# Two-layer decoder trunk: the seven products of a gate step paired by gate and up, their sums chained in place, down in two groups, and the parts of x in two rounds

## The reference, cut to what matters

```python
def swiglu(h, w_gate, w_up, w_down):
    return (jax.nn.silu(h @ w_gate) * (h @ w_up)) @ w_down

for l in range(DEPTH):
    x = x + 0.5 * swiglu(rms_norm(x, g_ffn1[l]), w_ffn1_gate[l], w_ffn1_up[l], w_ffn1_down[l])
    h = rms_norm(x, g_mix[l])
    # l == 0: x = x + conv_gating_mixer(h, ...)    l == 1: x = x + stick_breaking_mixer(h, ...)
    x = x + 0.5 * swiglu(rms_norm(x, g_ffn2[l]), w_ffn2_gate[l], w_ffn2_up[l], w_ffn2_down[l])
return rms_norm(x, g_final)
```

## Time and profile before

| | |
|---|---|
| median of 3 runs | 2059.07 us (2058.8 to 2063.93) |
| profiled execution, its own time | 2057.78 us |
| its span | 2056.1 us |
| PE busy, share of the span | 92% |
| DVE, ACT, POOL busy | 70%, 42%, 36% |
| mean granted PE clock | 0.956 of full |

### The profile page before, as it was taken

The page is one execution under the profiler, slowest core; times in us unless marked ns, Lnnn a source line. Parts: engine busy times, 40 slices in busy tenths (PEclk is TensorE's granted clock), DMA queues, the critical chain, the costliest instruction groups (busy, mean ns, idle before and its releaser), DMA issues.

```text
span 2056.1 us, 30552 instructions
## 1 busy us (share of the span) xinstructions
PE 1893.6 (92%) x11779; PEld 1696.5 (83%) x11779; DVE 1441.8 (70%) x1410; ACT 854.0 (42%) x1028; POOL 744.2 (36%) x551
## 2 busy tenths in 40 slices
PE   2999999989877999999599999989999969999998
PEld 2999988767657999988599998867888859999886
DVE  7778774579878778844977785453666697878642
ACT  3445442313235545522444543223555445544422
POOL 6454510331454555201645430040333274555003
PEclk6999999999988999999899999989999979999998
DMA  5788932222135888523479863223111147798321
GB/s 135 163 174 173 187 122 92 72 82 82 42 82 124 175 181 176 153 92 95 100 170 178 186 141 122 70 65 102 42 41 42 42 102 163 163 189 181 113 82 41
DMA packets 390330, 243.35 MB, mean 118 GB/s; under 512 B 13980, under 2 KB 358624, under 8 KB 390256
## 3 DMA queue, kind: packets, MB, share of 16 engines
q1 hardware_dynamic: 297088, 196.13, 32.1%
q0 software_dynamic: 93056, 46.22, 18.1%
q10 hardware_dynamic: 112, 0.03, 0.0%
HBM read 240.22 MB, written 2.10 MB: 118 GB/s over the span
## 4 chain that ended last, share of the span: by engine, by line
PE 69%; DVE 18%; issue 6%; POOL 4%; ACT 3%; DMA 0%; DVEq 0%; POOLq 0%; ACTq 0%
PE ps L360 23%; PE ps L362 22%; PE ps L361 22%; DVE w_lo L1361 5%; DVE y L1598 2%; ACT w_hi L978 2%; POOL ssq L1872 2%; POOL sq L1870 1%; PE ps L827 1%; PE ps L821 1%; DVE act_in L1397 1%; DVE xs_lo L1518 1%; DVE act_in L1402 1%; DVE x_sums L1501 1%; DVE w_lo L1332 1%
## 5 line engine op out<-in xcount | busy, mean ns | idle before, releaser
L360 PE MATMUL ps<-xs_hi,w_hi 128*128 128x256 f32 x2464 | 708.1, 287 | 110.6 <-DVE w_lo L1361 67.6
L361 PE MATMUL ps<-xs_lo,w_hi 128*128 128x256 f32 x2464 | 700.7, 284 | 0.0
L362 PE MATMUL ps<-xs_hi,w_lo 128*128 128x256 f32 x2464 | 700.4, 284 | 0.0
L1361 DVE TENSOR_TENSOR w_lo<-stage,w_hi 128x1024 fp32r<-128x1024 f32 x264 | 397.9, 1521 | 361.7 <-ACT w_hi L1051 200.8
L360 PEld LDWEIGHTS ps<-xs_hi,w_hi 128*128 128x128 f32 x2464 | 471.1, 191 | 122.3 <-DVE w_lo L1361 51.8
L361 PEld LDWEIGHTS ps<-xs_lo,w_hi 128*128 128x128 f32 x2464 | 471.4, 191 | 1.0 <-issue 1.0
L362 PEld LDWEIGHTS ps<-xs_hi,w_lo 128*128 128x128 f32 x2464 | 471.4, 191 | 0.0
L978 ACT ACTIVATE w_hi<-stage 128x1024 fp32r<-128x1024 f32 x176 | 182.7, 1057 | 306.0 <-PE ps L362 289.0
L1870 POOL TENSOR_TENSOR sq<-x_res 128x512 f32<-128x512 f32 x55 | 79.7, 1450 | 573.9 <-DVE x_res L1347 565.8
L360 PE MATMUL ps<-h_split,w_hi 128*128 128x512 f32 x704 | 278.8, 396 | 0.0
L361 PE MATMUL ps<-h_split,w_hi 128*128 128x512 f32 x704 | 278.7, 396 | 0.0
(11 more groups left out here) (229 smaller groups left out, 3024.2 us busy)
## 6 DMA issues: line engine op xcount, KB each, us to landing
stage<-in_w_ffn_gate_dram SPq DMA_DIRECT2D x176, 256.0 KB, 3.3
stage<-in_w_ffn_up_dram SPq DMA_DIRECT2D x176, 256.0 KB, 3.8
stage<-in_w_ffn_down_dram SPq DMA_DIRECT2D x176, 256.0 KB, 2.9
stage<-in_w_ffn_gate_dram POOLq DMA_DIRECT2D x88, 256.0 KB, 6.1
stage<-in_w_ffn_up_dram POOLq DMA_DIRECT2D x88, 256.0 KB, 6.8
stage<-in_w_qkv_dram SPq DMA_DIRECT2D x24, 512.0 KB, 4.9
sums<-in_w_ffn_gate_dram SPq DMA_DIRECT2D x44, 256.0 KB, 3.2
sums<-in_w_ffn_up_dram SPq DMA_DIRECT2D x44, 256.0 KB, 5.1
```

Source lines behind the costliest of these rows:

```text
L360: pe.matmul(to, a_hi, b_hi, start=start, stop=False, skip_group_check=True)
L361: pe.matmul(to, a_hi, b_lo, start=False, stop=False, skip_group_check=True)
L362: return pe.matmul(to, a_lo, b_hi, start=False, stop=stop, skip_group_check=True)
L1361: dve.tensor_tensor(w_lo[:, slot, :], src, w_hi[:, slot, :].bitcast(F32), ALU.subtract).then_inc(item_lo_made, 1)
```

## The change

It does the following things, together:

- **Output halves.** The second halving of a step is now gate against up, no longer first against last hidden channels; a step makes hidden tiles 2f and 2f+1. Each weight block is one DMA of 512 KB with rows of 1 KB, where there were two of 256 KB with rows of 512 B. The contraction is halved into even and odd tiles, so pairs of x are tiles 2k and 2k+1.
- **Order of the items:** T1, W11, T3, W21, T2, W22, T4. The gate half is complete after W22, so scale_gate and the silu come before T4 is done in all but the first step.
- **Sums.** T1 lies in one of two buffers (chain): SP loads W11's block there, POOL's DMA adds W12. T2 and T4 are made by POOL in the same buffer, in place, so each waits until the item before it in the chain has been split (item_lo_made). T3 is W12 plus W22 by an accumulating DMA.
- **Down in two groups of four output tiles.** An entry is two rows by four tiles (24 matmuls again). Entries 0 to 10 finish tiles 0 to 3, entries 11 to 21 tiles 4 to 7, and the residuals of the first group are added at entry 13. The high and low parts of hid are made anew in the second group, in two buffers that are parts S2 and S4 of x. PE's down loop is written out. The squares (POOL) or parts of x (ACT, DVE) for tiles 0 to 3 are made at entries 14 and 15.
- **Parts of x in two rounds.** x_pair makes five of seven parts; x_rest makes S2 and S4 for all four pairs afterwards.
- **Squares before an FFN** are taken by ACT (x_square, 128x512) and only added by POOL. Before the mixers and the final norm POOL still does both.

The diff, cut to its core:

```diff
-W11, W21, T1, T3, T2, W22, T4 = range(ITEMS)
+T1, W11, T3, W21, T2, W22, T4 = range(ITEMS)
-TAIL = [2, 3, 2, 2]
+GROUP = 4
+TAIL = 2
...
+        def gate_block(n, item, step):
+            w = ffn_weights[n][0 if item in (T3, W22) else 1]
+            odd = int(item in (W21, W22))
+            return w.rearrange("(k two p) f -> p two k f", two=2, p=P)[:, odd, :, bass.ds(step.count(2 * P, 0), 2 * P)]
...
 (load_ffn, SP)
+                for f in range(1, HF):
+                    if f > 1:
+                        sp.wait_ge(item_lo_made, lo0 + ITEMS * (f - 2) + T4 + 1)
+                        load_chain(n, Step(f))
+                    for item in (W11, T3, W21, W22):
+                        sp.wait_ge(item_lo_made, lo0 + ITEMS * (f - 1) + item + 1)
+                        if item == W21:
+                            sp.wait_ge(t4_made, n * HF + f)
+                        elif item == W22:
+                            sp.wait_ge(t2_made, n * HF + f)
+                        load_block(n, item, Step(f))
...
 (gate_first, PE)
+                pe.wait_ge(xs_lo_made, 10 * n + 2 * KH + 1)
+                gate_item(n, step, T2)
+                pe.wait_ge(xs_lo_made, 10 * n + 2 * KH + 2)
+                gate_item(n, step, W22)
                 pe.wait_ge(ssq_added, (norm + 1) * DT)
+                sum_squares(stats_bank(n)).then_inc(ssq_summed, 1)
+                gate_item(n, step, T4)
...
 (gate_mid and gate_step, ACT)
+                copy_r0(n, step)
+                hi(n, step, T2)
+                copy_v0(n, step)
+                hi(n, step, W22)
+                hi(n, step, T4)
...
+                if not step.first():
+                    hi(n, step, T3)
+                    hi(n, step, W21)
+                gate_mid(n, step)
+                copy_v(n, step)
+                hi(n, step.next(), T1)
+                if step.first():
+                    token_rms(NORM_FFN[n], stats_bank(n))
+                hi(n, step.next(), W11)
+                silu(n, step)
...
 (ffn(1) after down, ACT)
+                    first_hi(2, T1)
+                    first_hi(2, W11)
+                    x_pair(2, 2)
+                    first_hi(2, T3)
+                    first_hi(2, W21)
+                    x_pair(2, 3)
+                    x_rest(2)
+                    for j in range(GROUP, DT):
+                        x_square(2, j)
...
 (gate_step, DVE)
+                if not step.first():
+                    lo(n, step, T3)
+                    make_hid(n, Step(step.f - 1, step.i))
+                    lo(n, step, W21)
+                lo(n, step, T2)
+                lo(n, step, W22)
+                s57(n, step)
+                lo(n, step, T4)
+                c11(n, step)
+                c22(n, step)
+                lo(n, step.next(), T1)
+                c12(n, step)
+                if step.first():
+                    lo(n, step.next(), W11)
+                    c21(n, step)
+                    invert_rms(NORM_FFN[n])
+                    scale_gate(n, step)
+                else:
+                    scale_gate(n, step)
+                    lo(n, step.next(), W11)
+                    c21(n, step)
...
 (down, DVE)
+                for e in range(2, FT):
+                    if e + 1 < HF:
+                        scale_hid(n, e + 1)
+                    hid_lo(n, e)
+                    if e + 2 < FT:
+                        row_lo(n, e + 2)
+                    if e == 13:
+                        for at in range(GROUP):
+                            residual(n, at)
...
 (POOL)
+            def add_t4(n, step):
+                pool.wait_ge(item_lo_made, step.count(ITEMS, n * FFN_ITEMS + T2 + 1))
+                pool.wait_ge(raw_loaded[RAW_OF[W21]], step.count(16, raw_count(n, RAW_OF[W21]) + 16))
+                pool.tensor_tensor(step.chain(), step.chain(), raw(step, W21), ALU.add).then_inc(t4_made, 1)
+            def add_first(n):
+                add_t1(n, Step(0))
+                add_t3(n, Step(0))
+                if n:
+                    for j in range(GROUP):
+                        add_square(n, j)
+                add_t2(n, Step(0))
+                add_t1(n, Step(1))
+                for j in range(GROUP if n else 0, DT):
+                    add_square(n, j)
+                add_t4(n, Step(0))
+                add_t3(n, Step(1))
+            def gate_step(n, step):
+                add_t2(n, step)
+                if step.f < HF - 1:
+                    add_t1(n, step.next())
+                add_t4(n, step)
+                if step.f < HF - 1:
+                    add_t3(n, step.next())
```

More of the change, by code:

```diff
@@ L1416, in gate_step @@
             def gate_step(n, step):
+                if not step.first():
+                    lo(n, step, T3)
[5 more added lines that the diff above has]
+                lo(n, step, T4)
                 c11(n, step)
-                lo(n, step, W22)
-                lo(n, step, T4)
-                s57(n, step)
-                lo(n, step.next(), W11)
@@ L1926, in ffn @@
[L1926 to L1927 removed]
+                for f in range(1, HF):
+                    gate_step(n, Step(f))
+                clear_ssq(norm + 1)
+                if n == 1:
+                    add_first(2)
+                else:
+                    for j in range(DT if n < 3 else DT - 1):
+                        square_tile(norm + 1, j)
             def mask_diagonals(of, compare, count_sem):
@@ L1947, in _ @@
             clear_ssq(0)
-            squares(0, PAIRED, 0)
+            add_first(0)
             ffn(0)
@@ L1993, in _ @@
             clear_ssq(2)
-            squares(2, IN_ORDER, 1)
+            add_first(1)
             ffn(1)
@@ L2006, in _ @@
             clear_ssq(5)
-            squares(5, IN_ORDER, 3)
+            add_first(3)
             ffn(3)
```

843 lines of the change are left out of this document (413 added, 430 removed).

## The result

The changed kernel takes 1986.6 us (median of four runs, 1986.2 to 1989.7) against 2061.5 (2058.8 to 2065.4) on the same chip: ratio 0.9638, 95% interval 0.9617 to 0.966, 75 us less. The forecast was 1992, range 1966 to 2026. A later set on another chip (run e_again) gave 1986.8 for the same kernel (five runs, 1982.7 to 1987.9), but 2051.5 for the kernel before (nine runs, 2048.6 to 2057.6): ratio 0.9675, 95% interval 0.9657 to 0.9692, 65 us less. So the change is worth 65 to 75 us, and the kernel before varies more from set to set than the changed one does. The profiled execution spans 1984.7 us where that of before spans 2056.1, so there are 71.4 us to account for.

A forecast was written before the change was run, and what follows sets the result against it. PE was busy 1893.6 of 2056.1 us, so only idle time or slow clock, mostly in passages between stages, could be won. Terms summed to -67 from the profiled 2057.78, 1991, with the median 1.3 above: 1992, range 1966 to 2026.

The forecast's parts named there:

- The first case: Whole kernel: the gains and losses come as summed, 1970 to 2015 us; chance 0.72.
- Mixers' heads: FFN 0 to conv, FFN 2 to attention: early squares end PE's 9.1 us waits for ssq; 12 and 13 us won.
- FFN 1 to FFN 2: Passage with two x pairs made before down ends; stalls at T2 (5.7 us) and T4 remain; 14 us won, bounds 8 and 18.
- Mixer to FFN 3: Passage into FFN 3: pairs 0 and 1 made under the last output tiles, x_pair 3.4 us; 9 us won, bounds 3 and 15.
- Start: FFN 0's first step: first weights no longer wait behind POOL's squares; ends about 62 instead of 68.7; 7 us won.
- Gate steps: Later FFN steps: POOL's sums stand apart where DVE has slack, so later stalls go; 12 us won, bounds 3 and 14.
- first steps: After step 0: silu(0) ahead of T3's high part makes PE's stall about 4.1 against 2.6; four times, 6 us lost.
- Down: Doubled hid work is covered except in entries 14 and 15, mainly FFN 1's; 7 us lost, bounds 0 and 12.
- DMA: SP and POOL queues: fewer, larger DMAs for the same bytes; DMA does not get worse, no term in the sum.
- the second: POOL's sums hold DVE in the steps: no gain there and 0.5 us more in each of 40, 2024; chance 0.12.
- The third: FFNs' first steps win nothing because T2 and T4 wait behind squares on ACT and POOL, 2029; chance 0.07.
- The fourth: T3's accumulating DMA lands later than its 14 us in the steps, each us then costing 40: slower; chance 0.04.

The follow-up runs named there:

- e_again: The changed kernel run once more, unaltered, beside the combined kernel on another chip: 1986.8 us (1982.7 to 1987.9).
- e_late: The changed kernel with tiles 0 to 3's residuals and all that followed at entries 13 to 15 moved behind the last down matmul: 2021.8 us.
- e_pool_sq: The changed kernel with the squares in front of the FFNs made on POOL again instead of by ACT: 2008.1 us.
- e_start: The changed kernel with pair 1 of x made ahead of T1's high part at the start, on ACT and DVE: 1981.6 us.
- e_squares: The changed kernel with ACT's squares in front of the FFNs moved into ACT's idle gaps, and POOL's adds with them: 1984.0 us.
- e_tail: The changed kernel with tiles 4 and 5 of down's row 20 taken before tile 4 of row 21: 1982.8 us.
- e_rows: The changed kernel with each SP block load as two DMAs of 256 KB with packets of 512 bytes: 2014.9 us.
- e_rows_order: The e_rows kernel, with SP loading W22 ahead of W21: 1996.9 us.
- e_pool_more: The changed kernel with two further unused sums of 512 columns on POOL behind T2's sum in each of steps 1 to 10: 2009.6 us.
- e_first: The changed kernel with step 1's T3 and W21 high parts ahead of silu(0) on ACT, T3's low part ahead of DVE's reciprocal: 1982.9 us.
- e_best1: The changed kernel with e_first, e_start and e_tail joined, squares and T2's sum placed, and step 1's T3 DMA issued earlier: 1952.5 us.

## Why the prediction was right

The first case came: 1986.6 for 1992, and the sum of -67 stands at -71 in the spans. The mechanisms came too, place by place. That the sum is so near is partly luck: the gate steps gave 10 us more than forecast and down 2.5 us less loss, FFN 1 and FFN 2 near 3 us more, and the start, the end and the way to FFN 3 some 11 us less. By its terms:

- **Mixers' heads**, -12 and -13: -11.0 and -13.2. PE's wait for ssq is gone and the clock stays at 1.00, as it said. e_late shows the cause: with the tiles late they lose 8.6 and 10.5 us again.
- **FFN 1 to FFN 2**, -14: -15.1. The stall at T2 is 4.0 us for 5.7. The second, at T4, did not appear: T2 and W22 run partly at half clock behind the first stall and give T4 its time. e_late gives 9.6 of it to the early pairs.
- **Mixer to FFN 1**, -7: -8.6. **Mixer to FFN 3**, -9: -4.6, within its bounds of 3 and 15. The step that was off is the pair at 3.4 us: pairs 0 and 1 take 2.5 us each, but pair 2 of FFN 3 takes 7.7 us (1608.29 to 1616.04), four of its six instructions at 1.54, 1.48, 1.48 and 2.83 us beside POOL's adds of squares and T2's sum. PE waits 7.5 us. Pair 2 of FFN 1 is held as long (584.45 to 592.27), but PE waits only 2.2 us for it. This was the lower bound's own condition, and e_pool_sq shows the kind of loss. One part of pair 2 on DVE, and what POOL does meanwhile:

```profile
1612.56 2.83 DVE L1575 SCALAR_TENSOR_TENSOR xs_lo<-x_res,params,xs_hi 128x512 fp32r<-128x512 f32 x1
```

```profile
1606.71 5.64 POOL L1990 TENSOR_TENSOR ssq<-ssq,copies 128x512 f32<-128x512 f32 x4 [6.28 <-ACT copies L1201]
1612.43 2.41 POOL L1978 TENSOR_TENSOR chain<-chain,stage 128x1024 f32<-128x1024 f32 x1
```

- **Start**, -7: -2.5. The count took T1's DMA as one wait of ACT, but all of pair 1 stood behind it (6.4 us; e_start wins 4.5 to 5.3 back), and ACT's eight squares and POOL's eight adds stood in front of T2 and T4 (e_squares: 4.4).
- **End**, -6: -4.2 for down and end of FFN 3 together, in which down lost 1.1 or more; e_late takes 7.6 back.
- **Gate steps**, -12, and **first steps**, +6, so -6 together: -16.1, the term that was off most. The stalls came as forecast: those of steps 2 to 10, 11.7 us, went altogether, and step 1's grew from 9.8 to 13.5, +3.7 for +6. (The working of +6 has a slip: it puts T3's low part 8.6 us after step 0 with 5.7 us of work for PE, which is a stall of 2.9 and not of 4.1; measured were 2.9 to 4.0.) That is 8 us of idle time less. The other 8 lie beside the stalls, in time that isn't recorded as idle. One stall of the kernel before, in FFN 3:

```profile
1795.81 0.28 PE L362 MATMUL ps<-xs_hi,w_lo 128*128 128x256 f32 x1
1797.56 0.39 PE L360 MATMUL ps<-xs_hi,w_hi 128*128 128x256 f32 x1 [1.47 <-DVE w_lo L1361]
1797.79 0.28 PE L361 MATMUL ps<-xs_lo,w_hi 128*128 128x256 f32 x1
```

  Starts are 0.12 us apart elsewhere; here they are 1.75 apart, of which 1.47 are idle, and then 0.23: 0.27 us are lost on top. Over all starts of steps 1 to 10 such long distances at granted clock 1.00 cost 9.1 us in the kernel before (72 of them) and 0.5 in the changed one (4). Those at half clock cost 4.6 and 4.3, so the clock gave next to nothing here, and the slower pace of the last section, in one FFN of four, took 1.8 back. I had counted idle time alone. In e_again's profile of the changed kernel the same steps win only 9.3 us: two FFNs ran at the slower pace instead of one, and half clock followed the stall of step 1 in all four FFNs instead of two (7.2 us for 4.3). So some 6 of the 16 us may be chance; of the kernel before there is one profile only.
- **Down**, +7: +4.5 in FFN 0 to 2 (124.1, 124.5 and 124.0 us for 122.7, from the last gate matmul's end to the last down matmul's), but not for the reason given. I put the 5 us at entries 14 and 15, where ACT and DVE make a pair besides; no gap is there. The loss is for the most part one wait of 1.1 us in every FFN, with the time lost beside it, at the last row: two buffers for hid, and only six matmuls between the coming free of row 21's buffer and its need. e_tail removes it (122.7, 123.2 and 122.7). The size was right by luck.
- **DMA**, costed at nothing. The sum is not hurt by that, but the reason was thin. I weighed time per packet and left out what is chained to a landing. e_rows shows that the change with SP's block loads at the old size would have been worth 47 us, not 75: the larger loads carry 28, about half of them through the ring of T4's sum, W21's load, W22's load and T2's sum (13.7 us in the gate steps, e_rows_order).

Of the rivals, the second (POOL's sums hold DVE in the steps) had its mechanism right. The sums do hold DVE, for 2.87 us at scale_gate in place of 1.23. They fall where there is slack, and e_pool_more shows that 4.2 us more of POOL in a step uses it up in two FFNs of four. The rule that the prediction takes from the Trainium skill (SBUF — State Buffer, Who interferes with whom), that a DVE instruction with two SBUF inputs and a GpSimd instruction that reads SBUF keep each other out, agrees with the rows of e_squares: 2.62 us for 0.48 beside a sum of 2.46. The third was half true in FFN 0 and FFN 3, not in FFN 1 and 2. The fourth looked at the wrong DMA for the later steps: T3's lands in 9.1 us of the 14 allowed, while W22's load, which the prediction never named, had 0.8 us left in one step and none in ten. In step 1 T3's DMA does count: it is what lay beneath the stall (e_first). The outer bounds were added up a little off: from 1992 they give 2042 and 1955, not 2041 and 1956.

## What to carry to other kernels

Count for each engine what stands in front of the late thing, and then what stands behind that: the stall at T3 had ACT's wait for scale_gate on top and the issue of a DMA on POOL beneath it, and taking the upper one away won 3.5 us and moved the stall to the next item. With the lower one gone as well it fell to 1.4 us and less. Together with the edits of the start, the squares and down that made 35. Where POOL and DVE share SBUF, look where each POOL operation will start once its inputs are there, and try a wait that gives it a better place (e_best1 has such waits, but not alone, so their own worth is not shown). And before a DMA is called hidden, follow the ring that it closes (who frees its buffer, what is queued ahead of it, who waits for its landing) and write down its slack: here it was 0.8 us or less in a step of 20, and twice the number of loads with rows half as long cost 28 us. Last, a stall costs more than its idle time (0.27 us more in the rows above), and two profiles of one kernel can differ by 4 us in one stage; profile the unaltered kernel twice before small terms are explained.

## What the runs showed of the hardware that was not expected

The same matmuls of 256 columns, at granted clock 1.00 and with no idle time, run at two paces. Windows of the changed kernel's later steps, FFN 1 and FFN 2, in its first profile and then in e_again:

```profile
640.00:820.00 180.00, 180.00 (x1519) 180.00 (x1519) 142.08 (x128) 88.17 (x102) 71.37 (x35) 1.00 0.74 175
1000.00:1180.00 180.00, 180.00 (x1503) 180.00 (x1502) 140.65 (x127) 87.55 (x100) 71.81 (x35) 1.00 0.73 174
```

```profile
640.00:820.00 180.00, 180.00 (x1503) 180.00 (x1502) 140.11 (x125) 86.76 (x100) 73.21 (x35) 1.00 0.73 172
1000.00:1180.00 180.00, 179.87 (x1516) 179.66 (x1515) 140.86 (x128) 87.73 (x101) 73.03 (x35) 1.00 0.74 176
```

1519 (or 1516, with 0.13 us idle) or 1503 matmuls in 180 us, 0.1185 or 0.1198 us each. (From start to start it is 0.1187 and 0.1200; the counts take in a matmul or two at the edges.) No records are missing: each profile has all 1704 of the stretch from T4 on. FFN 1 had the faster pace in one execution and the slower in the other, FFN 2 the reverse, with the same instructions. An FFN is worth 2.2 us less or more by that, and four of them 9. What sets the pace was not tried and stays open.

Half clock behind a stall is as fickle. Step 1 of FFN 0 in the two profiles:

```profile
66.60:89.70 23.10, 20.19 (x171) 19.99 (x170) 17.97 (x17) 10.45 (x13) 8.51 (x5) 1.00 0.74 173
```

```profile
65.50:90.80 25.30, 21.64 (x170) 21.43 (x169) 18.90 (x16) 9.69 (x12) 11.22 (x5) 0.93 0.78 182
```

The first has a stall of 2.9 us and stays at clock 1.00; the second has one of 3.7 us, and 3.4 us at half clock follow it. It is not the length of the stall alone: in the kernel before the stall of 2.6 us in step 1 of FFN 0 was followed by 3.4 us at half clock. A difference of 4 us in one FFN's steps between two kernels says nothing until it is put beside this.
